# A two-layer hybrid decoder trunk on one core: x scaled and turned by transposes, first casts moved ahead, S5 products placed between long ones

## What is computed

```python
def rms_norm(x, g):
    y = xf * lax.rsqrt(jnp.mean(xf * xf, axis=-1, keepdims=True) + NORM_EPS)
    return (y * g).astype(x.dtype)

h = rms_norm(x, norm_g)
proj = jnp.einsum('bsd,de->bse', h, w_in)        # u_lru, u_s5, qkv_ret, q_nsa, kv_nsa, bg, gate paths, merge
y_lru = rg_lru_mixer(u_lru, ...)                 # log_a = -8 * r * softplus(-lam)
y_s5 = s5_mixer(u_s5, ...)                       # parameters from lambda, log_dt: exp, cos, sin; then a linear scan
...
return x + jnp.einsum('bsd,de->bse', merged, w_out)
```

## Time and profile before

| what | before |
|---|---|
| median of 3 runs | 763.61 us (762.98 to 764.16) |
| the profiled execution, its own time | 762.22 us |
| its span | 760.4 us |
| PE, busy | 740.1 us (97%), 6046 matmuls |
| DVE, busy | 486.6 us (64%) |
| ACT, busy | 418.8 us (55%) |
| POOL, busy | 304.3 us (40%) |
| DMA | 126.85 MB, 167 GB/s in the mean |
| granted clock, mean over the span | 0.997 |

### The profile page before, as it was taken

How to read it: one execution, slowest core, us unless ns; L and a number is a source line. 1 busy time by engine, 2 the same in 40 slices (tenths; PEclk the granted TensorE clock), 3 DMA queues, 4 the chain that set the end, 5 groups by cost and what they waited for, 6 DMA issues and landing times.

```text
span 760.4 us, 14637 instructions
## 1 busy us (share of the span) xinstructions
PE 740.1 (97%) x6046; PEld 630.6 (83%) x6046; DVE 486.6 (64%) x773; ACT 418.8 (55%) x673; POOL 304.3 (40%) x135
## 2 busy tenths in 40 slices
PE   7999899999999999999999998999999999999996
PEld 7888789889888888878898887888898788888785
DVE  4989977583679453534778898576564966153344
ACT  6686624546653656455458664354465546655441
POOL 3000000005778976788200000000555989766740
PEclk9999999999999999999999999999999999999999
DMA  8559464564355545555545775466635456545541
GB/s 257 149 168 283 157 224 145 176 235 139 92 157 166 169 140 166 169 164 167 147 97 167 254 189 191 144 217 194 193 98 152 136 149 186 164 135 175 170 135 55
DMA packets 87009, 126.85 MB, mean 167 GB/s; under 512 B 22072, under 2 KB 32672, under 8 KB 86944
## 3 DMA queue, kind: packets, MB, share of 16 engines
q1 hardware_dynamic: 86768, 125.89, 55.0%
q10 hardware_dynamic: 176, 0.04, 0.0%
HBM read 124.86 MB, written 1.05 MB: 166 GB/s over the span
## 4 chain that ended last, share of the span: by engine, by line
PE 85%; issue 7%; POOL 4%; DVE 1%; ACT 1%; ACTq 0%; POOLq 0%; DVEq 0%
PE proj L1695 62%; POOL w_lo L685 4%; PE M L1690 4%; PE proj L1732 4%; PE proj L1736 2%; PE M L2078 2%; PE proj L1763 2%; PE M L1883 1%; PE M L1894 1%; PE M L1851 1%; PE proj L1769 1%; PE proj L1785 1%; PE M L2052 1%; PE M L1955 1%; PE M L2047 1%
## 5 line engine op out<-in xcount | busy, mean ns | idle before, releaser
L685 POOL TENSOR_TENSOR w_lo<-raw,w_hi 128x1024 fp32r<-128x1024 f32 x112 | 287.9, 2601 | 408.4 <-ACT w_hi L707 385.3
L707 ACT ACTIVATE w_hi<-raw 128x1024 fp32r<-128x1024 f32 x200 | 206.5, 1054 | 111.9 <-PE proj L1695 64.7
L1695 PE MATMUL proj<-w_hi,h_hi 128*128 128x512 f32 x544 | 216.4, 398 | 1.5 <-POOL w_lo L685 1.5
L1695 PE MATMUL proj<-w_hi,h_lo 128*128 128x512 f32 x544 | 212.2, 390 | 0.0
L1695 PE MATMUL proj<-w_lo,h_hi 128*128 128x512 f32 x544 | 211.9, 389 | 0.0
L1695 PEld LDWEIGHTS proj<-w_hi,h_hi 128*128 128x128 f32 x544 | 102.2, 188 | 24.3 <-issue 2.7
L1695 PEld LDWEIGHTS proj<-w_hi,h_lo 128*128 128x128 f32 x544 | 102.1, 188 | 21.7
L1695 PEld LDWEIGHTS proj<-w_lo,h_hi 128*128 128x128 f32 x544 | 102.2, 188 | 20.4 <-issue 0.5
L1282 DVE TENSOR_TENSOR w_lo<-raw,w_hi 128x1024 fp32r<-128x1024 f32 x80 | 95.0, 1221 | 33.2 <-ACT w_hi L707 32.8
L1695 PE MATMUL proj<-w_hi,ys_hi 128*128 128x512 f32 x128 | 50.9, 397 | 0.5 <-POOL w_lo L685 0.5
L1695 PE MATMUL proj<-w_hi,ys_lo 128*128 128x512 f32 x128 | 50.0, 390 | 0.0
(11 more groups left out here) (335 smaller groups left out, 1200.5 us busy)
## 6 DMA issues: line engine op xcount, KB each, us to landing
raw<-in_w_in SPq DMA_DIRECT2D x152, 512.0 KB, 4.2
raw<-in_w_branch SPq DMA_DIRECT2D x32, 512.0 KB, 3.9
raw<-in_w_out SPq DMA_DIRECT2D x16, 512.0 KB, 4.6
raw<-in_s_w_glu SPq DMA_DIRECT2D x8, 512.0 KB, 4.8
raw<-in_w_in SPq DMA_DIRECT2D x8, 256.0 KB, 3.1
merged<-in_nsa_ck_w SPq DMA_DIRECT2D x4, 512.0 KB, 7.1
mt<-in_nsa_ck_w SPq DMA_DIRECT2D x4, 512.0 KB, 9.0
merged<-in_nsa_cv_w SPq DMA_DIRECT2D x4, 512.0 KB, 4.5
```

The lines of the kernel that those rows point to most:

```text
L685: nc.gpsimd.tensor_tensor(w_lo[:, slot(s, l), 0:n * w], raw[:, u % N_RAW, 0:n * w], w_hi[:, slot(s, l), 0:n * w].bitcast(f32), ALU.subtrac ...
L707: i = nc.scalar.activation(out_, in_, func, **kw)
L1695: last = mm(dst, left[i], right[j], start=start and n == 0, stop=stop and n == 2, skip_group_check=True)
```

## The change

It has five parts.

1. x is scaled by DVE into `merged` in two halves of 512 columns (`scaled_x`, two signals for each half of the tokens) in place of a scaled identity, and turned by `nc.tensor.transpose` with the plain identity. The squares' unused output goes to `h_full` instead of `merged`. In layer 0 the mean of the first 128 tokens no longer waits for the second (`input_mean`), and TensorE turns them before the vectors.
2. In layer 0, SP loads weight unit 0 ahead of the vectors and the constants behind unit 3. ACT casts unit 0 first and the others between pairs of `h_hi`; `parameters` is split in three and put between. DVE does the four lows of `u_s5` in a row, then `h_lo`, now straight from M, then `parameters_c`; `h_full` waits for `h_lo`.
3. `input_chunk` takes, per unit, the products with `w_hi`, then those with `w_lo` of the unit before.
4. The softplus moves behind the lows of `gate_lru`.
5. The S5 products stand between units of `nsa_kv` and `gate_s5`.

```diff
         def scaled_x(dve, l, t):
             Layer(dve, l).wait_ge(rstd, t + 1)
-            nc.vector.tensor_scalar(diag[:, t, :], ident, st[:, 2 + t:3 + t], None, ALU.mult).then_inc(diag_done, 1)
+            for half in range(2):
+                e = slice(512 * half, 512 * half + 512)
+                nc.vector.tensor_scalar(merged[:, t, e], x[:, t, e], st[:, 2 + t:3 + t], None, ALU.mult).then_inc(x_scaled, 1)
         def turn_x(pe, l, t):
-            Layer(pe, l).wait_ge(diag_done, t + 1)
             for k in range(KD):
+                if k % 4 == 0:
+                    Layer(pe, l).wait_ge(x_scaled, 2 * t + k // 4 + 1)
-                last = nc.tensor.matmul(M[:, k // 2, at:at + P], x[:, t, k * P:(k + 1) * P], diag[:, t, :], start=True, stop=True)
+                last = nc.tensor.transpose(M[:, k // 2, at:at + P], merged[:, t, k * P:(k + 1) * P], ident)
...
+                        prefetch(0)
                         sp.wait_ge(cleared, 1)
                         load_vectors(queue, 0, VECTORS_A)
-                        prefetch(0)
-                        prefetch(1)
+                        for u in range(1, N_RAW):
+                            prefetch(u)
                         queue.dma_start(const[:, P:N_CONST], a["constants"][:, P:N_CONST]).then_inc(const_loaded, 16)
-                        prefetch(2)
-                        prefetch(3)
...
                     act.wait_ge(vec_ready, 1)
                     if l == 0:
-                        parameters(0)
                         cast_input(0, 0)
-                        cast_input(0, 1)
                     for k in range(KD):
+                        if l == 0 and k == 0:
+                            parameters_exp(0)
+                        if l == 0 and k and k % 2 == 0:
+                            cast_input(0, k // 2)
                         if k % 2 == 0:
                             act.wait_ge(xT_done, k // 2 + 1)
                         run(h_hi[:, k, :], M[:, k // 2, (k % 2) * T:(k % 2 + 1) * T], ACT.Copy, hhi_done,
                             scale=vec[:, V_NORM + k:V_NORM + k + 1])
+                        if l == 0 and k == 1:
+                            parameters_mag(0)
                     if l == 0:
-                        cast_input(0, 2)
-                        cast_input(0, 3)
+                        parameters_sin(0)
                     for k in range(KD):
+                        if k % 2 == 0:
+                            act.wait_ge(hlo_done, k + 2)
                         run(h_full[:, k, :], ...)
...
                     if l == 0:
-                        mean_of_first_half(vector, 0, link)
-                        for t in range(TT):
-                            mean_square(vector, 0, t)
+                        input_mean(vector, 0, link)
+                        scaled_x(vector, 0, 0)
+                        input_mean(vector, 1, link)
                         expand_dt(vector, 0)
+                        scaled_x(vector, 0, 1)
                         vector.wait_ge(ident_loaded, 16)
                         keep_vectors(vector, 0)
-                        for t in range(TT):
-                            scaled_identity(vector, 0, t)
                         parameters_a(0)
+                        parameters_e(0)
                         parameters_b(0)
                         input_lo(0, 0)
                         input_lo(0, 1)
-                        parameters_c(0)
                     input_lo(l, 2)
                     input_lo(l, 3)
-                    for k in range(0, KD, 2):
-                        v.tensor_tensor(flat(h_lo[:, k:k + 2, :]), flat(h_full[:, k:k + 2, :]), ...
+                    for k in range(KD):
+                        v.scalar_tensor_tensor(h_lo[:, k, :], M[:, k // 2, (k % 2) * T:(k % 2 + 1) * T], ...
+                    parameters_c(l)
                     parameters_d(l)
...
+                        for u in range(KD // 2):
+                            pe.wait_ge(hi_done, u + 1)
+                            half_products(u, w_hi, u == 0)
+                            if u:
+                                wait_low(pe, u - 1)
+                                half_products(u - 1, w_lo, False)
+                        wait_low(pe, KD // 2 - 1)
+                        half_products(KD // 2 - 1, w_lo, False)
...
                         tensor.wait_ge(ident_loaded, 16)
+                        turn_x(tensor, 0, 0)
                         turn_vectors(tensor, 0)
-                        for t in range(TT):
-                            turn_x(tensor, 0, t)
+                        turn_x(tensor, 0, 1)
...
-                    chunk("nsa_kv")
+                    chunk("nsa_kv", 0)
                     state_inputs(1)
+                    chunk("nsa_kv", range(2, 3))
                     own_outputs(0)
+                    chunk("nsa_kv", range(3, 4))
                     state_outputs(0)
                     compress(0, "ck")
                     chunk("gate_s5", 0)
                     chunk_kernels(1)
                     hidden_T(0, "ck")
-                    chunk("gate_s5", 1)
+                    chunk("gate_s5", range(2, 3))
                     own_outputs(1)
+                    chunk("gate_s5", range(3, 4))
                     state_outputs(1)
```

More of the change, by code:

```diff
@@ L239, in hybrid_trunk @@
         sc = sb("sc", [P, 7168])
-        diag = sb("diag", [P, TT, P])
+        blank = sb("blank", [P, P])
         half_pi = sb("half_pi", [P, 1])
@@ L1051, in _ @@
                     if l + 1 < DEPTH:
-                        parameters(l + 1)
+                        parameters_exp(l + 1)
+                        parameters_mag(l + 1)
+                        parameters_sin(l + 1)
                         cast_input(l + 1, 0)
@@ L1082, in parameters_a, with parameters_e @@
                         v.tensor_scalar(S(11), lam_r, -1e-4, None, ALU.min)
+                    def parameters_e(s):
+                        stage = Layer(vector, s)
                         stage.wait_ge(dt_exp, 1)
@@ L1755, in input_chunk, with half_products @@
                         ps = pr("u_s5")
[L1756 to L1766 removed]
+                        def half_products(u, w, first):
+                            for k in (2 * u, 2 * u + 1):
+                                if w is w_hi:
+                                    pe.wait_ge(hhi_done, k + 1)
+                                for m in range(4):
+                                    e = slice((k % 2) * 512 + m * P, (k % 2) * 512 + (m + 1) * P)
+                                    mm(ps[:, m * T:(m + 1) * T], w[:, slot(u, l), e], h_hi[:, k, :],
+                                       start=first and k % 2 == 0 and m % 2 == 0, stop=False, skip_group_check=True)
+                        for u in range(KD // 2):
[6 more added lines that the diff above has]
+                        half_products(KD // 2 - 1, w_lo, False)
+                        for k in range(KD):
+                            pe.wait_ge(hlo_done, k + 1)
                             for m in range(4):
```

112 lines of the change are left out of this document (55 added, 57 removed).

## The result

| what | before | after |
|---|---|---|
| median | 763.42 us (762.98 to 764.16, 4 runs) | 753.30 us (752.94 to 754.07, 4 runs) |
| the profiled execution | 762.22 us (span 760.4) | 753.15 us (span 751.3) |
| TensorE (PE), busy | 740.1 us, 6046 matmuls | 736.1 us, 6014 matmuls |

The changed kernel takes 0.9865 of the time of the kernel before (95% interval 0.9844 to 0.9886): 10.1 us less between the medians, 9.1 us less between the two profiled executions.

The account below looks back on a forecast made before the run. TensorE bounds the kernel almost end to end. Head 2.3 + S5 bursts 5.3 + seam 0.9 = 8.5 us, so 753.7 for the profiled execution; plus 1.4 to the median, 755.1 us; range 753.3 to 759.5, forecast's own 753.3 to 757.2.

Parts of the forecast that it names:

- Rival 1: Clock low through the whole input chunk and again at the seam: gain only 5.5 us, so 758.1; chance 0.15.
- block D: Layer 1, one instruction packet: 126 `state_inputs(1)` records and 2 long products, 2.35 us of work; no stop expected.
- Rival 2: TensorE's stops are not fetching, or have other room, and move with the S5 bursts: gain 3.2 us, 760.4; chance 0.07.
- rival 4: Each new short block finds its packet behind loads: 765.5 us at delay 5.3; fetch family 0.09, of which 0.05 slower.
- B, C: Short blocks: 113 `state_outputs` plus 15 compression records, 2.55 us, layer 0; 3 long plus 125 `state_inputs(0)`, 2.5 us, layer 1.
- E: Layer 1, a short block of 86 + 32 + 9, 4.2 us of work; 0.3 us kept for a stop.
- Term of the bursts: S5 products of both layers: long products between them remove most of 5.78 us of stops; gain 5.3, bounds 5.8 and -4.1.
- Term of the head: Start of layer 0: first high product near 12.6 instead of 15.74 us; gain 2.3 us, bounds 3.1 and 1.0.
- Term of the seam: Between the layers: x turned by single-record transposes, 16 records; gain 0.9 us, bounds 1.3 and -0.8.
- New waits of that order: Reordered S5 products: earlier `state_inputs(1)` has 0.75 us spare, `own_outputs(1)` waits for DVE's kernels; cost 0, at most 1 us.
- softplus: nothing: Softplus, some 2.9 us on DVE, moves to where DVE stood idle 7.56 us; no effect on time.
- Rival 3: Head's gain is lost before 75 us in the DVE and load chain feeding `nsa_kv`: gain 6.2, 757.4; chance 0.08.

Follow-up runs that it names:

- second profile: The changed kernel, unaltered, run again and its slowest execution profiled, which had half clock in the head; median 753.25 us.
- the two looks: The kernel before, unaltered, profiled a second and a third time: 760.46 and 761.65 us.
- the earlier cast: The changed kernel with ScalarE's cast of weight unit 0 moved ahead of its wait for the vectors: 752.13 us.
- the second look: The kernel before, unaltered, in its third profile: 761.65 us.

## Why the prediction was right in kind and short in size

**The bound and the mechanism** were right. TensorE bound the kernel, "issue" was a wait for instructions in packets of 256, and the forecast places were the right ones: the only stop left is in block D. Rival 1 (the clock) did not come about: in the profile it is 1.00 through the input chunk and the seam, and where it did fall (second profile, 14 to 18 us) it cost some 1.0 us in the head and nothing in the seam. Rival 2 (stops are no matter of fetching) is refuted by the stops that moved with 16 matmul records fewer and with 72 and 208 instructions more, and rival 4 (each short block finds its packet behind loads) by four of five blocks that were passed without a stop. The Trainium skill, "Runtime: NRT & Kernel Launch", Instruction fetch mechanics, gives blocks of 256 instructions, which all these counts agree with; its statement that the fetch is hidden fails in the bursts of this kernel: blocks that held 2.2 to 3.4 us of work ended in stops, though others of 1.9 to 2.6 us (B, C) did not; none that held 3.6 us or more did.

**The step that failed most: the base.** The sum gave 753.7 for the profiled execution, and I then added the 1.4 us by which that execution lay under the median of before. This took the offset as something that the change would leave in place. In the changed kernel it was 0.15 us (753.15 and 753.30). That is 1.2 of the 1.8 us; the other 0.6 are the terms of the sum, which gave 8.5 us where 9.1 came. The kernel before varies from 760.5 to 767.7 over all its runs here, the changed one by 1.1 us (752.9 to 754.1 in eight runs). Between three profiles of the kernel before the stops account for most of the difference, and the change removes them; half clock in the head has a part in the longer times. Which of the two made the 1.4 stays open, since the executions behind that median left no profile. 753.7 would have been 0.4 off; 755.1 was 1.8 off. The range went wrong with it: its upper bounds together, 10.2 us off 763.61, give 753.4 (the prediction has 753.3), and the gain from there was 10.3, more than all of them.

**Term of the bursts: 5.3, measured 6.0.** The stops were taken at their printed idle time, 5.78, and cost 7.4. Against that stand 0.8 for block D, from which I kept nothing (I kept 0.2 for B and 0.3 for E, which cost nothing), and 0.8 for the changes between short and long products, which the sum did not have. The delay of 2.35 us from one block to the next is the least one: at that very place it was 2.7 and 2.9 us in the two looks, it was 3.2 in block D (438.55 to 441.74, data DMA at 0.46 of its share from 438.5 to 440) and 3.5 in the kernel with 24 empty instructions. "The packet queues behind loads" was read from two places, and it stays an argument: the two looks repeat the long delay (about 4.6 us in both, DMA at 0.92 and 0.96 ahead of it) and the short one (DMA at 0.06 and 0.07), but no run changed the loads alone.

**Term of the head: 2.3, measured 2.5,** by two errors that cancel. The clock did not fall in the profiled execution, where 3.1 was the forecast; but the first product came at 12.88, not 12.6, since the vectors were loaded late (VectorE waited 0.69 us for them, so `vec_ready` came at 11.1 and not at 10.8), and the second and third group waited another 0.60 and 0.22. That this came near the forecast, which had half clock in it, is luck. With half clock the gain is 1.8 (28.26 to 26.47), within the bounds. The Trainium skill, "TensorE: Matmul & The Clock Gate", Part 4, was cited against turning by transposes; the four executions with matmuls instead all have a clock of 0.998 or 0.999, but so have all four with transposes and the earlier cast, so these runs do not decide it.

**Term of the seam: 0.9, measured 0.6.** VectorE was on time: the second half is scaled from 2.35 us behind the last product, as forecast. The eight transposes from there to the first product took 1.17 us instead of the 0.11 each that the row inside a stream of long products gives.

**New waits of that order: 0,** right, but for one step: "softplus: nothing". The 0.75 us that `state_inputs(1)` had to spare were counted in the kernel before; TensorE comes 2.5 us earlier from the head besides. With the softplus at its old place ScalarE's copy came too late by 0.7 us; with it moved, in both profiles, it did not. That was read in one profile, whose whole time was no longer.

**Rival 3** (the head's gain is lost before 75 us) did not come about: TensorE's S5 transposes ahead of `nsa_kv` start at 65.00 instead of 67.50, so the 2.5 us still stood there.

## What to carry to other kernels

Count instructions as well as time: where a few hundred short matmuls follow each other, the places where TensorE stops are fixed by the instruction count from the program's start, and any edit ahead of them, even a removed one, moves them. Put slow work into every stretch of 256 instructions (3.6 us of it sufficed here), and take the loss of a stop from start to start. Before carrying an offset between a profile and a median over to the changed kernel, ask what the executions differ in; if it is something that the change removes, the offset may go with it.

## What the runs showed of the hardware

- **Empty instructions can make a kernel faster.** 208 of them between long products cost 0.0 us where they stand and took 3.0 us off the kernel, by moving the borders of instruction packets.
- **The delay of a packet is no constant.** At the same record of the same program the stop was 2.25, 1.70 and 1.70 us in three executions, and at another 2.29, 1.30 and 1.30, but at a third 0.38, 0.71 and 0.95. The data DMA ahead of the first was at 0.93, 0.92 and 0.96 of its share and ahead of the third at 0.05, 0.06 and 0.07, so this share tells a long delay from a short one, but not one execution from another.
- **A clock column of 1.00 is not always full speed.** The warm-up matmuls on zeros ran 12 in 2 us, then 15 in the changed kernel (in the first profile of before 19 of the same ran from 4 to 6 us), at a granted clock of 1.00 throughout:

```profile
4.00:6.00 2.00, 2.00 (x12) 2.00 (x11) 0.00 (x0) 1.89 (x3) 2.00 (x1) 1.00 1.00 363
6.00:8.00 2.00, 2.00 (x15) 1.84 (x14) 0.54 (x3) 1.95 (x8) 0.71 (x2) 1.00 1.07 344
```

  In another execution of the same kernel they ended 1.1 us sooner (6.96 instead of 8.03), so the step up comes at no fixed time after their start.
- **Half clock costs by what runs in it.** From 11 to 14.4 us in the kernel before it lay on the turning of x, ahead of a wait, and cost nothing: the input chunk is over at 28.26 with it and at 28.28 in an execution without. On the first products it cost 0.5 us in the second look and some 1.0 us in the changed kernel's second profile, and behind 4.57 us of idle time some 2 us.
